# Second block of a two-block transformer kernel: other banks for the absorbed queries and the scores, mLSTM distance on ScalarE, paired small products, squares beside the way out

## What is computed

```python
def hybrid_layer(x, w_in, ..., cos, sin):
    h = rms_norm(x, norm_w)
    p = h @ w_in
    (dsa_q, dsa_ckv, dsa_krope, idx_q, idx_k, idx_w, dsa_z,
     sb_q, sb_k, sb_v, sb_z,
     ml_qk, ml_v, ml_i, ml_f, ml_o, ml_z, merge) = jnp.split(p, splits, axis=-1)
    y_a = dsa_attention(...)              # 8 heads, 64 best keys by index score
    y_b = stick_breaking_attention(...)   # 8 heads
    h_c = mlstm_chunkwise(...)            # 4 heads
    y_c = head_layer_norm(h_c, ml_norm_w) * jax.nn.sigmoid(ml_o)
    branches = jnp.stack([y_a * silu(dsa_z), y_b * silu(sb_z), y_c * silu(ml_z)], axis=2)
    proj = jnp.einsum('bsgc,gcd->bsgd', branches, w_branch)
    gates = jax.nn.sigmoid(merge.reshape(bsz, seq, N_BRANCHES, D_MODEL))
    mixed = jnp.sum(gates * proj, axis=2)
    return x + mixed @ w_out
```

## Time and profile before

| what | value |
|---|---|
| median of 3 runs | 2646.95 us (2642.33 to 2650.3) |
| the profiled execution | 2648.71 us |
| its span, first to last instruction | 2646.9 us |
| mean granted TensorE clock | 0.975 of 2.4 GHz |
| TensorE busy | 2473.6 us, 93% of the span |
| VectorE / ScalarE busy | 61% / 40% |
| HBM read | 346.4 MB, 131 GB/s over the span |
| second block | from 1862 us to the end, two layers of 386 us |

### The profile page before, as it was taken

How to read it: one execution, slowest core, us unless ns; L and a number is a source line. 1 busy time by engine, 2 the same in 40 slices (tenths; PEclk the granted TensorE clock), 3 DMA queues, 4 the chain that set the end, 5 groups by cost and what they waited for, 6 DMA issues and landing times.

```text
span 2646.9 us, 35085 instructions
## 1 busy us (share of the span) xinstructions
PE 2473.6 (93%) x14142; PEld 2096.9 (79%) x14142; DVE 1601.5 (61%) x2815; ACT 1049.2 (40%) x1767; POOL 0.2 (0%) x4
## 2 busy tenths in 40 slices
PE   6999998997989999999999889899999799999798
PEld 5888886875668888778888667899889688989777
DVE  8777756268477774477333555555757557648456
...
## 3 DMA queue, kind: packets, MB, share of 16 engines
...
HBM read 346.41 MB, written 1.05 MB: 131 GB/s over the span
## 4 chain that ended last, share of the span: by engine, by line
PE 86%; DVE 7%; ACT 4%; issue 2%; DMA 1%; SPq 0%; DVEq 0%; ACTq 0%
PE ps L418 24%; PE ps L420 24%; PE ps L419 24%; PE ps L515 2%; ACT w_hi L997 2%; PE ps L595 1%; PE ps L597 1%; PE ps L596 1%; PE ps L639 1%; DVE w_lo L1456 1%; DVE small L1618 1%; PE ps L626 1%; PE ps L928 1%; PE ps L746 1%; DVE uT L1482 1%
## 5 line engine op out<-in xcount | busy, mean ns | idle before, releaser
L997 ACT ACTIVATE w_hi<-ring 128x1024 fp32r<-128x1024 f32 x504 | 533.5, 1060 | 1275.2 <-PE ps L420 1203.1
L1456 DVE TENSOR_TENSOR w_lo<-ring,w_hi 128x1024 fp32r<-128x1024 f32 x504 | 615.8, 1223 | 657.8 <-ACT w_hi L997 655.8
L418 PE MATMUL ps<-u_hi,w_hi 128*128 128x512 f32 (+1 forms) x1744 | 636.8, 365 | 30.4 <-DVE u_lo L1471 27.9
L420 PE MATMUL ps<-u_hi,w_lo 128*128 128x512 f32 (+1 forms) x1744 | 634.0, 364 | 0.0
L419 PE MATMUL ps<-u_lo,w_hi 128*128 128x512 f32 (+1 forms) x1744 | 630.4, 361 | 0.0
L418 PEld LDWEIGHTS ps<-u_hi,w_hi 128*128 128x128 f32 x1744 | 330.7, 190 | 87.1 <-issue 34.1
L419 PEld LDWEIGHTS ps<-u_lo,w_hi 128*128 128x128 f32 x1744 | 330.5, 190 | 54.2 <-issue 0.5
L420 PEld LDWEIGHTS ps<-u_hi,w_lo 128*128 128x128 f32 x1744 | 330.8, 190 | 53.5
L418 PE MATMUL ps<-uh,w_hi 128*128 128x256 f32 x1184 | 349.4, 295 | 21.9 <-ACT merge L1320 12.4
L1444 DVE CUSTOM_DVE_ANT_0 waste<-ring,condb,cols 128x1024 f32<-128x1024 f32 x280 | 346.5, 1279 | 7.9 <-DMA ring<-in_wk 7.9
L419 PE MATMUL ps<-ul,w_hi 128*128 128x256 f32 x1184 | 336.6, 284 | 0.0
...
## 6 DMA issues: line engine op xcount, KB each, us to landing
ring<-in_wk SPq DMA_DIRECT2D x324, 1024.0 KB, 4.8
...
condb<-in_crow SPq DMA_DIRECT2D x1, 1024.0 KB, 5.4
out_t<-uT SPq DMA_DIRECT2D x1, 1024.0 KB, 3.9
...
```

The costliest lines, as they stand in the source:

```text
L418: mm(bank, hi, x_hi, start=first, stop=False)
L420: return mm(bank, lo, x_hi, start=False, stop=last)
L997: f(half_hi(K, 0, HALF), ringed(n, K % 2 * HALF, (K % 2 + 1) * HALF), ACT.Copy).then_inc(whi_ready, 1)
L1456: tt(half_lo(K, 0, HALF), ringed(HALF_SLOT[K], K % 2 * HALF, (K % 2 + 1) * HALF), half_hi(K, 0, HALF).bitcast(F32), ALU.subtract).then_inc ...
```

## The change

Nine edits, in the second block and what follows it:

- Absorbed queries go to ps[2]/ps[3], ahead of their column, and are evacuated ahead of it; a new semaphore `qabs_free`.
- `ml_dist` is gone from DVE. ScalarE computes it as two Relu with the negated column as bias (gcol is written negated), and exp behind them; DVE's `lows(1)` stands behind ml_weigh and ml_divide. The small operations of ml_divide do both token halves in one.
- The stick-breaking scores are made once, in one of four banks (SB_BANK), and the cumulative sum is added to them in place.
- Rotations and index scores are issued in pairs behind every other column; the gate rows come one or two columns earlier.
- The first half of merge column 16 is issued ahead of the softmax units, so that each unit has the other half beside it and the last one none; DVE's and ScalarE's part of it moves from even to odd units.
- The output products move from slots 2 and 3 of the first branch to slot 3 and to slot 0 of the second.
- On the way out ScalarE squares each piece of hT beside the next column; DVE sums the first five squares, and TensorE adds that sum and the sixth ahead of the last column, the other two behind it.
- The weight conversions of the last column of a layer move behind the norm (ScalarE) and behind ul (DVE).
- The output DMA goes in two halves.

```diff
+SB_BANK = [5, 6, 2, 3]
...
     assert n == NSLOTS
-    sp.wait_ge(t_ready, T_READY_END)
-    sp.dma_start(out, uT[:, 0:KC * S]).then_inc(out_done, 16)
-    sp.wait_ge(out_done, 16)
+    for half in range(2):
+        sp.wait_ge(t_ready, T_READY_END - (1 - half) * KC // 2)
+        n = half * KC // 2 * S
+        sp.dma_start(out[:, n:n + KC // 2 * S], uT[:, n:n + KC // 2 * S]).then_inc(out_done, 16)
+    sp.wait_ge(out_done, 32)
...
     H = a = v = parts = norms = 0
-    sq_seen = ulo_seen = y_seen = h_seen = y_sums = 0
+    sq_seen = ulo_seen = y_seen = h_seen = y_sums = h_sums = 0
...
+    def h_sums_early():
+        nonlocal h_sums
+        pe.wait_ge(rstd_ready, norms)
+        h_sums += 1
+        pe.wait_ge(b2["hsum"], h_sums)
+        mm(bankN[:, 0:S], tab("ones"), tile(sq2, 0), start=True, stop=False)
+        pe.wait_ge(sq_ready, sq_seen + ADDED + 1)
+        mm(bankN[:, 0:S], tab("ones"), tile(sq2, ADDED), start=False, stop=False)
+    def h_sums_late():
+        nonlocal norms, sq_seen
+        for c in range(ADDED + 1, KC):
+            pe.wait_ge(sq_ready, sq_seen + c + 1)
+            last = mm(bankN[:, 0:S], tab("ones"), tile(sq2, c), start=False, stop=c == KC - 1)
+        last.then_inc(ss_done, 1)
+        norms += 1
+        sq_seen += KC
...
-    def softmax_units(specs, beside=None):
+    def softmax_units(specs, beside=None, free=None):
...
             pe.wait_ge(p_ready, units + u + 1)
+            if u == 0 and free:
+                pe.wait_ge(*free)
...
         first = a
-        norm_sum(S, sq_ready, sq_seen, src=sq2, stride=S)
-        sq_seen += KC
+        if lay:
+            h_sums_late()
+        else:
+            norm_sum(S, sq_ready, sq_seen, src=sq2, stride=S)
+            sq_seen += KC
...
                 last.then_inc(b2["ckvt_done"], 1)
-            if 3 <= t < 11:
+            if t in (4, 6, 8, 10):
                 pe.wait_ge(a_free, first + t - 1)
+                rotate("swap_half", turning[t - 4])
                 rotate("swap_half", turning[t - 3])
-            if t >= 11:
+            if t in (12, 14, 16):
+                index_scores(t - 12)
                 index_scores(t - 11)
-        values(2, uh2, ul2, S, lambda t: index_scores(6 + t))
+        values(2, uh2, ul2, S)
+        index_scores(6)
+        index_scores(7)
...
-        def z_scores(h, bank, go, end):
-            r = slice(64 * (h % 2), 64 * (h % 2) + 64)
-            mm(bank[:, 0:S], tile(sbk, h // 2, 0, P)[r, :], tile(sbq, h // 2)[r, :], start=go, stop=False,
-               skip_group_check=True)
-            return mm(bank[:, S:S + P], tile(sbk, h // 2, P, P)[r, :], tile(sbq, h // 2, P, P)[r, :],
-                      start=False, stop=end, skip_group_check=True)
         def sb_first(h):
-            n = 8 * lay + h
...
                 pe.wait_ge(a_free, first + 17)
-            if n >= 2:
-                pe.wait_ge(b2["sp"], n - 1)
-            z_scores(h, ps[5 + h % 2], True, True).then_inc(b2["z_full"], 1)
+            elif h == 2:
+                pe.wait_ge(v_free, v)
+            elif h >= 4:
+                pe.wait_ge(b2["lga"], 8 * lay + h - 3)
+            r = slice(64 * (h % 2), 64 * (h % 2) + 64)
+            bank = ps[SB_BANK[h % 4]]
+            mm(bank[:, 0:S], tile(sbk, h // 2, 0, P)[r, :], tile(sbq, h // 2)[r, :], start=True, stop=False,
+               skip_group_check=True)
+            mm(bank[:, S:S + P], tile(sbk, h // 2, P, P)[r, :], tile(sbq, h // 2, P, P)[r, :],
+               start=False, stop=True, skip_group_check=True).then_inc(b2["z_full"], 1)
         def sb_second(h):
-            n = 8 * lay + h
-            if h == 0:
-                pe.wait_ge(v_free, v)
-            if n >= 2:
-                pe.wait_ge(b2["lga"], n - 1)
-            z_scores(h, ps[2 + h % 2], True, False)
-            pe.wait_ge(b2["sp"], n + 1)
-            w = ps[2 + h % 2]
+            pe.wait_ge(b2["sp"], 8 * lay + h + 1)
+            w = ps[SB_BANK[h % 4]]
...
         for h in range(DSA_HEADS):
+            r = slice(64 * (h % 2), 64 * (h % 2) + 64)
+            if h >= 2:
+                pe.wait_ge(b2["qabs_free"], 8 * lay + h - 1)
+            mm(ps[2 + h % 2][:, 0:S], wuk[r, h // 2 * P:(h // 2 + 1) * P], tile(dq, h // 2)[r, :],
+               start=True, stop=True).then_inc(b2["qabs"], 1)
             project(1, S, uh2, ul2, S)
-            r = slice(64 * (h % 2), 64 * (h % 2) + 64)
-            mm(bank_a()[:, 0:S], wuk[r, h // 2 * P:(h // 2 + 1) * P], tile(dq, h // 2)[r, :],
-               start=True, stop=True).then_inc(b2["qabs"], 1)
-        absorbed = a
...
         pe.wait_ge(b2["qk_silu"], 2 * (lay + 1))
+        pe.wait_ge(b2["qabs_free"], 8 * (lay + 1))
...
-        pe.wait_ge(a_free, absorbed)
...
                     nk = P * (qt + 1)
-                    if (h, qt) == (1, 0):
-                        pe.wait_ge(b2["mbr"], 4 * (lay + 1))
...
         def merge_column(u):
-            half_column(bank_a() if u % 2 == 0 else bankA[(a - 1) % 2], u % 2, S, uh2, ul2, S)
-        softmax_units(specs, merge_column)
+            if u < 2 * KC - 1:
+                half_column(bankA[(a - 1) % 2] if u % 2 == 0 else bank_a(), 1 - u % 2, S, uh2, ul2, S)
+        half_column(bank_a(), 0, S, uh2, ul2, S)
+        softmax_units(specs, merge_column, (b2["mbr"], 4 * (lay + 1)))
...
             for half in range(4):
-                if p == 0 and half >= 2:
-                    for h in range(4 * half - 8, 4 * half - 4):
+                if (p, half) in ((0, 3), (1, 0)):
+                    for h in range(4 * p, 4 * p + 4):
...
             weights(H)
+            if m == KC - 1:
+                h_sums_early()
...
                 column(bank_v(), S, uh2, ul2, S, b2["mixlo"], KC * (lay + 1))
-    norm_sum(S, sq_ready, sq_seen, src=sq2, stride=S)
+    h_sums_late()
...
                 rms_inverse(tile(prob, 0), ps[7][:, 0:S], DSA_R).then_inc(hr_ready, 1)
-            if t == 5:
+            if t == 4:
...
                     act.wait_ge(b2["sp"], n - 1)
-                step(f(sx(h % 2, 1), ps[5 + h % 2][:, 0:384], ACT.Abs))
+                step(f(sx(h % 2, 1), ps[SB_BANK[h % 4]][:, 0:384], ACT.Abs))
...
         for h in range(DSA_HEADS):
+            act.wait_ge(b2["qabs"], 8 * lay + h + 1)
+            f(tile(qabs, h), ps[2 + h % 2][:, 0:S], ACT.Copy).then_inc(b2["qabs_free"], 1)
             tiles(1, lambda t, bank, h=h: f(tile(merge, h), bank[:, 0:S], ACT.Sigmoid))
-            act.wait_ge(b2["qabs"], 8 * lay + h + 1)
-            f(tile(qabs, h), bankA[a % 2][:, 0:S], ACT.Copy).then_inc(a_free, 1)
-            a += 1
...
         act.wait_ge(b2["gcol_ready"], lay + 1)
-        f(small[:, SM_LN + 40:SM_LN + 48], small[:, SM_GCOL + 8:SM_GCOL + 16], ACT.Exp,
-          scale=-1.0).then_inc(b2["mx"], 1)
+        f(small[:, SM_LN + 40:SM_LN + 48], small[:, SM_GCOL + 8:SM_GCOL + 16], ACT.Exp).then_inc(b2["mx"], 1)
...
         for h in range(ML_HEADS):
-            act.wait_ge(b2["mdist"], 4 * lay + h + 1)
+            n = 4 * lay + h
+            act.wait_ge(b2["ms_full"], n + 1)
+            if h >= 2:
+                act.wait_ge(b2["msw"], n - 1)
+            g = SM_GCOL + h
+            f(mx(h % 2, 0, 0, S), ps[2 + h % 2][:, 0:S], ACT.Relu, bias=small[:, g:g + 1]).then_inc(act_step, 1)
+            steps += 1
+            step(f(mx(h % 2, 0, S, P), ps[2 + h % 2][:, P:S], ACT.Relu, bias=small[:, g + 4:g + 5]))
...
         def beside(u):
-            if u >= 2 and u % 2 == 0:
-                merge_raw(15 + u // 2)
+            if u < 16 and u % 2:
+                merge_raw(16 + u // 2)
...
                 used()
-                if p == 0 and half == 3:
-                    branch_high(2, b2["dbr"], 0)
-                    branch_high(2, b2["dbr"], 1)
-                if p == 1 and half == 0:
-                    branch_high(2, b2["dbr"], 2)
-                    branch_high(2, b2["dbr"], 3)
+                if p == 1 and half < 2:
+                    branch_high(2, b2["dbr"], 2 * half)
+                    branch_high(2, b2["dbr"], 2 * half + 1)
...
         for m in range(KC):
-            used()
-        v += KC
-    squares(S, v_free, v - KC, 1, sq2, S)
+            if m < KC - 1:
+                used()
+            else:
+                H += 1
+                act.wait_ge(half_done, H)
+            v += 1
+            act.wait_ge(v_free, v)
+            f(tile(sq2, m), tile(hT, m), ACT.Square).then_inc(sq_ready, 1)
...
         first = a
-        a += 81
+        a += 73
+        if lay:
+            low()
...
                 head_norm(ckv[:, :], col("kvn", lay), tile(prob, 0))
-            if 3 <= t < 11:
-                rope(xs[t - 3], trig[:, 0:S], trig[:, S:2 * S], tile(tmp, t % 2))
-            if t == 7:
+            if t in (4, 6, 8, 10):
+                for j in (t - 4, t - 3):
+                    rope(xs[j], trig[:, 0:S], trig[:, S:2 * S], tile(tmp, j % 2))
+            if t == 5:
...
```

(60 more changed lines are left out.)

8 lines of the change are left out of this document (4 added, 4 removed).

## The result

The changed kernel took **2583.89 us** (median of 4 runs, 2578.39 to 2585.99) against 2647.96 us for the kernel before (4 runs): a ratio of 0.9756, 95% interval 0.9731 to 0.978. The forecast was 2585, with 2573 to 2604 as its range. The profiled execution took 2583.04 us, with a span of 2581.2 us at a mean granted clock of 0.982 (0.975 before).

A forecast was written before the change was run, and what follows sets the result against it. TensorE's waits and slow-clock matmuls were taken as the bound. Two layers of 28.4 us gave 56.9, boundaries 4.6, together 61.5 us off 2648.7: 2587.2, with the median 1.8 lower at 2585 us, range 2573 to 2604.

The forecast's parts named there:

- What bounds the kernel: Whole kernel: TensorE holds 86% of the chain; time is gained only where it waits, runs slow or issues less.
- Absorbed queries: Second block, columns around the absorbed queries: own banks remove seven waits of 0.88 us, gain 6.2 us a layer.
- mLSTM: mLSTM stretch: distance on ScalarE and ml_weigh ahead of low() end the output waits, gain 17.4 us a layer.
- The end of the softmax units at 0: Softmax units: filling the old 2.02 us wait balances a new 1.2 us wait at the last unit, gain 0.
- rival (c): Second block: more gained, as second scores were not free and slow matmuls after idle time vanish; 2575 us, chance 0.08.
- Scores in place: Stick-breaking scores: second sets mostly overlapped already, so only the one standing alone is gained, 0.85 us a layer.
- Index pairs and rotations: Index scores and rotations: paired index products overlap on opposite row halves, gain 2.9 us a layer; rotations gain 0.
- Branches: Branches: moving the output products removes the 1.4 us wait on L1983; 1.1 us remain as gain a layer.
- Boundaries: Step between layers and end: early squares gain 2.4 and 1.8 us, output in halves 0.4, together 4.6 us.
- (a): mLSTM loop: ScalarE becomes the bound through two table loads a head; 16 us more, 2601 us, chance 0.15.
- (b): Index scores: pairs do not overlap because their products leave through banks in turn; 5.7 us lost, 2591 us, chance 0.08.
- (d): Whole kernel: slower than before because a denser TensorE is granted less clock; 2655 us, chance 0.02.

The follow-up runs named there:

- the control: The kernel before itself, unchanged, run again for a second profiled execution; 2651.47 us, ratio 1.0008 to the kernel before.
- e8: The changed kernel with the absorbed queries back in the two A banks, taking turns with the columns; 2596.13 us, ratio 0.9783 to the kernel before.
- e4: The kernel before with the mLSTM edit alone (Relu on ScalarE, low() last); 2617.28 us, ratio 0.9894 to the kernel before.
- e6: The changed kernel with the second set of stick-breaking scores issued again; 2585.41 us, ratio 0.9741 to the kernel before.
- e7: The changed kernel with two more ScalarE table loads around the Relus of each mLSTM head; 2599.5 us, ratio 0.9789 to the kernel before.
- e5: The changed kernel with index heads ordered 0, 2, 1, 3, so paired products share a row half; 2588.61 us, ratio 0.9751 to the kernel before.

## Why the prediction was right, step by step

- **What bounds the kernel** held: every gain sat where TensorE waited or ran slow, and the two stretches without either are at 1.00 and never idle in the changed kernel.
- **Absorbed queries**: right, 6.2 us of waits a layer, as forecast. The stretch gained 6.9 and 6.8 us against the first profile of before and 6.3 against the control; e8 gives back 7.0 and 6.8.
- **mLSTM**: the stretch is 37.0 us, forecast 37.2. A layer gained 17.6 us against the first profile of before, 15.0 and 16.6 against the control, and e4 shows 14 to 17 from the edit alone; 17.4 were forecast. The reason given was half right. The prediction told of two causes (no handover to DVE, and `ml_weigh` ahead of `low()`); only the second gains more than 0.3 us. It priced the Relus at 0.67 us; they took 0.83 by their records, 0.37 apart at their starts. Against the rule weighed there, that relu belongs on VectorE (the Trainium skill's "ScalarE: Activation LUTs", section "Rules for kernel authors"): in this case the engine made 0.27 us a layer, in ScalarE's favour, and the rule decided nothing.
- **The end of the softmax units at 0**: this is the step that failed, by 2 us a layer. I saw the old wait of 2.02 us filled, but did not carry on that matmuls behind it were slow. That sat in rival (c): the 8 us behind that mark had a clock of 0.79 before and have 1.00 now. Some 1.5 us of the 2 are this slow piece; the control's layer 1, which had the wait and no slow piece, took 45.67 us against 45.1 to 45.2 now, so 0.5 belongs to the stretch itself. The mLSTM edit alone did not do it: e4 keeps the wait and shows 47.15 and 47.20 us. A shorter wait makes the slow piece rarer, and does not exclude it. Behind the old wait of 2 us it came in five layers of six (before, control, e4). Behind the 0.6 us that are left it came in one of eighteen, layer 0 of e6, where the stretch took 46.77 us:

```profile
2109.35:2117.35 8.00, 8.00 (x43) 6.54 (x44) 3.38 (x14) 3.88 (x11) 0.00 (x0) 0.79 0.13 33
```

- **Scores in place**: overlap was right (e6), the gain undersized: 1.35 against 0.85 a layer. The 16 instructions given for the second sets of a pair of heads are 8 in the trace; the sum does not use them.
- **Index pairs and rotations**: the index pairs gained 2.8 us a layer against 2.9. The reason was half right, since a pair costs what a single did, but only 1.5 us of that is overlap and the rest came with fewer turns. The whole stretch gained 3.2 and 4.8: 0.4 us lie outside the index scores, where I had put the rotations at 0, and 1.5 in layer 0 is a slow piece at the first columns that the first profile of before has and the control has not.
- **Branches**: 0.7 against 1.1 a layer. The waits on L1983 are gone (2.9 us in both layers), but those behind DVE's conv grew from 0.9 to 1.8 us in all, and six of 0.3 to 0.4 us stayed.
- **Boundaries**: 2.7 and 3.1 against 2.4 and 2.2; the output in halves was undersized (1.1 against 0.4).
- **Rivals**: (a) did not occur, but e7 gives its mechanism and a price of 11 us in the stages against the forecast's 16; (b) did not occur, and e5, which takes the overlap away by another way, cost 3 us rather than 6; (c) occurred in part; (d) did not: the mean clock rose.
- **The total** is nearer than its parts: 61.5 was forecast, the stages gave 70.9 against the first profile of before and 63.5 against the second. That the median moved by 64.1 is in part luck: gains that were too small in the sum (softmax, scores, boundaries) stand against an mLSTM gain that is below it beside the control, and the first block scatters by some us besides. A sum made against one profile inherits how many slow matmuls that execution happened to have.
